# One fused two-block program on one core: modulation rows moved between the projection units, stick-breaking norms moved into the differential attention, opening reordered

## The reference

```python
h = rms_norm(x, g_attn)                      # opening
proj = h @ w_in                              # six outputs of width 512: dq dk dv sq sk sv
dq, dk = rms_norm(dq, qn_g), rms_norm(dk, kn_g)
w = softmax(dq1 dk1 + bias) - lam * softmax(dq2 dk2 + bias)
o_da = rms_norm(w @ dv, subln_g)             # differential attention, 4 heads
o_sb = rms_norm(stick_breaking(sq, sk, sv), sb_out_g)     # 8 heads
x = x + concatenate([o_da, o_sb]) @ w_o
x = x + hier_moe(rms_norm(x, g_ffn), ...)    # 32 experts
# second block
mod = silu(c) @ w_ada + b_ada                # 1024 x 6144, for c and for c_ctx
... modulate(...), Fourier mix, latent attention, feed-forward ...
```

## Time and profile before

| | |
|---|---|
| median of 3 runs | 1538.5 us |
| the profiled execution | 1539.48 us; span 1537.7 us; 1.8 us lie around the span |
| TensorE busy | 1434.8 us (93%) |
| VectorE, ScalarE busy | 526.2 us, 427.2 us |
| mean granted TensorE clock | 0.976 |
| bytes moved | 313.87 MB, mean 204 GB/s |

### The profile page before, as it was taken

The page is one execution under the profiler, slowest core; times in us unless marked ns, Lnnn a source line. Parts: engine busy times, 40 slices in busy tenths (PEclk is TensorE's granted clock), DMA queues, the critical chain, the costliest instruction groups (busy, mean ns, idle before and its releaser), DMA issues.

```text
span 1537.7 us, 16696 instructions
## 1 busy us (share of the span) xinstructions
PE 1434.8 (93%) x6918; PEld 910.6 (59%) x6918; DVE 526.2 (34%) x965; ACT 427.2 (28%) x725; POOL 33.0 (2%) x84
## 2 busy tenths in 40 slices
PE   6999998796999999998999879999999999999996
PEld 5877754484454445444454343555447888887885
DVE  3235557535311211121121045267344222223233
ACT  5237644512100000000200143156334222223222
POOL 0001100000000000000000021000000000000000
PEclk9999999698999999999999999999999999999998
DMA  7421069325699999999999751200004223212201
GB/s 293 135 89 55 1 256 427 165 107 221 273 426 429 427 427 428 427 399 409 394 403 416 286 195 59 79 28 1 0 0 181 93 110 110 89 75 110 83 0 55
DMA packets 30196, 313.87 MB, mean 204 GB/s; under 512 B 3908, under 2 KB 3908, under 8 KB 12456
## 3 DMA queue, kind: packets, MB, share of 16 engines
q1 hardware_dynamic: 22312, 295.06, 46.9%
q10 hardware_dynamic: 6656, 13.53, 2.8%
q0 software_dynamic: 1152, 4.19, 0.8%
HBM read 298.35 MB, written 14.43 MB: 203 GB/s over the span
## 4 chain that ended last, share of the span: by engine, by line
PE 79%; DMA 14%; DVE 3%; ACT 2%; issue 1%; POOL 0%; SPq 0%; ACTq 0%; DVEq 0%; POOLq 0%
PE ps L55 76%; DMA ring<-in_w 7%; DMA B<-in_w 3%; DMA ring<-in_w_ada 2%; PE ps L1061 2%; DMA X<-in_x 1%; PE ps L805 0%; DMA B<-yslots,SMI 0%; POOL B L524 0%; PE ps L571 0%; DVE TMP L1855 0%; DVE WL L1650 0%; DVE X L1653 0%; ACT WH L1559 0%; PE ps L768 0%
## 5 line engine op out<-in xcount | busy, mean ns | idle before, releaser
L55 PE MATMUL ps<-ring,B 128*64 128x512 f32 (+2 forms) x880 | 263.6, 600 | 16.4 <-DMA ring<-in_w 14.7
L55 PEld LDWEIGHTS ps<-ring,B 128*64 128x64 f32 (+1 forms) x880 | 88.2, 147 | 137.9 <-issue 133.6
L55 PE MATMUL ps<-B 128*64 128x512 f32 (+5 forms) x440 | 146.6, 562 | 7.7 <-DMA ring<-in_w 5.9
L55 PE MATMUL ps<-B,B 128*128 128x128 f32 (+1 forms) x1072 | 141.5, 293 | 3.9 <-DVE B L1910 3.9
L55 PE MATMUL ps<-XH,WH 128*128 128x512 f32 (+1 forms) x368 | 140.9, 383 | 1.3 <-DVE XL L1650 0.7
L55 PEld LDWEIGHTS ps<-B,B 128*128 128x128 f32 (+1 forms) x1072 | 123.4, 191 | 28.6 <-issue 24.2
L55 PE MATMUL ps<-XL,WH 128*128 128x512 f32 (+1 forms) x368 | 139.7, 380 | 0.0
L55 PE MATMUL ps<-XH,WL 128*128 128x512 f32 (+1 forms) x368 | 139.7, 380 | 0.0
L1559 ACT ACTIVATE WH<-ring 128x2048 fp32r<-128x2048 f32 x33 | 63.2, 1916 | 168.1 <-PE ps L55 168.1
L1650 DVE TENSOR_TENSOR WL<-ring,WH 128x2048 fp32r<-128x2048 f32 x33 | 75.7, 2293 | 95.4 <-ACT WH L1559 95.4
L1390 ACT ACTIVATE TMP<-ps 64x512 f32<-64x512 f32 x32 | 19.0, 595 | 238.1 <-PE ps L55 238.0
(11 more groups left out here) (293 smaller groups left out, 2012.2 us busy)
## 6 DMA issues: line engine op xcount, KB each, us to landing
ring<-in_w SPq DMA_DIRECT2D x65, 2048.0 KB, 16.9
B<-in_w SPq DMA_DIRECT2D x24, 2048.0 KB, 17.4
ring<-in_w_ada SPq DMA_DIRECT2D x12, 2048.0 KB, 12.6
ring<-in_w_gu SPq DMA_DIRECT2D x11, 2048.0 KB, 8.3
ring<-in_w_in SPq DMA_DIRECT2D x7, 2048.0 KB, 8.8
TO<-in_w SPq DMA_DIRECT2D x7, 2048.0 KB, 16.9
ring<-in_w_down SPq DMA_DIRECT2D x5, 2048.0 KB, 7.2
yslots<-TMP ACTq DMA_DIRECT2D x64, 128.0 KB, 9.2
```

The source lines that it names most:

```text
L55: return e.matmul(o, l, r, start=first, stop=last, skip_group_check=True)
```

## The change

It has four parts.

1. The twelve modulation blocks leave the differential attention. A table `ADA_AT` puts block b behind projection unit n, and its four transposes into unit n+1 (two thirds or three quarters through). They use PSUM bank 7 instead of 5 and 4; `sk` and `dv` therefore use banks 4, 5, 6, 3.
2. The loads of `w_in`, `w_ada` and `w_o` are interleaved in one list and use slots 0, 1, 2 and 4, in the fixed order `early`. The zero source for the overflow slots moves from slot 4 to `B1`, and ScalarE issues its 15 copies two per unit instead of one.
3. The stick-breaking norms (`so_square`, `wo_norm`, `so_norm`, `so_gain`, `so_high`, `so_low`), `od_low(0..1)`, and the first two output weight splits stand inside the passes of the differential attention.
4. In the opening, VectorE squares row tiles 1 and 3, tile 2 is scaled on ScalarE, the transposes go by row tile instead of by column chunk, the first weight split stands ahead of `HH`, the two bias-row matmuls stand behind unit 0, and the parameter load moves from ScalarE's queue to SyncE's, behind `X`.

```diff
+    ADA_AT = {1: 0, 2: 1, 3: 2, 5: 3, 6: 4, 7: 5, 9: 6, 10: 7, 11: 8, 12: 9, 13: 10, 14: 11}
+    early = [0, 1, 2, 4, 1, 0, 2, 4, 0, 2, 1, 4, 2, 1, 0, 4, 1, 2, 1, 2]
...
+        e.dma_start(PRM[:, 0:N_PARAM], I["PRM"]).then_inc(prm_in, 16)
+        for i in range(4):
             load(i)
...
+        def ada_product(b):
+            w = slot(I_ADA[b], 8, 512)
+            if b:
+                e.wait_ge(ada_mod, 2 * b - 1)
+            else:
+                e.wait_ge(cs_set, 4)
+                e.wait_ge(brow_cp, 2)
+            e.wait_ge(slot_in[where[I_ADA[b]]], landed[I_ADA[b]])
+            for c in range(8):
+                m = mm(e, P[7][32 * (c % 4):32 * (c % 4) + 32, :], CS[:, c, :], w[:, c, :], c < 4, c >= 4)
+            m.then_inc(ada_mm, 1)
+
+        def ada_turn(b):
+            e.wait_ge(ada_row, b + 1)
+            for j in range(4):
+                t = e.transpose(P[7][:, 128 * j:128 * j + 128], AD[b % 2][:, 128 * j:128 * j + 128], ident)
+            t.then_inc(ada_T, 1)
...
+                    if c == 5 and n - 1 in ADA_AT:
+                        ada_turn(ADA_AT[n - 1])
...
+            if n in ADA_AT:
+                ada_product(ADA_AT[n])
...
             if i >= 2:
                 qt, h = DA[i - 2]
-                if i - 2 <= 11:
-                    e.wait_ge(ada_mod, 2 * (i - 2) + 1)
...
+                if i in (2, 4, 6, 8):
+                    wo_norm((i - 2) // 2)
+                if i in (10, 14):
+                    turn_rows((i - 10) // 4)
...
-            if i >= 15:
-                wo_norm(i - 15)
-            if i in (14, 15, 17):
-                turn_rows((14, 15, 17).index(i))
+        turn_rows(2)
         out_projection(0)
-        wo_norm(3)
         turn_rows(3)
...
+            if i in (4, 6, 8, 10):
+                so_gain((i - 4) // 2)
+            if i in (6, 8, 10, 12):
+                so_low((i - 6) // 2)
...
+            if i in (12, 16):
+                od_low((i - 12) // 4)
+            if i in (13, 15):
+                wo_low((i - 13) // 2)
```

More of the change, by code:

```diff
@@ L176, in body @@
     ce = small[:, 0:16].rearrange("p (k r) -> p k r", r=2)
-    AD = [B2[:, 2048 + 512 * g:2560 + 512 * g] for g in range(3)]
+    AD = [TMP[:, 2048 + 512 * g:2560 + 512 * g] for g in range(2)]
     E = [[TMP[:, 1024 * k + 512 * j:1024 * k + 512 * j + 512] for j in range(2)] for k in range(3)]
@@ L284, in body @@
     SG = [TMP[:, 2048 + 512 * k:2560 + 512 * k] for k in range(2)]
-    items = [I["w_in"][m] for m in PROJ]
-    I_ADA = len(items)
-    items += [I["w_ada_2"][b] for b in range(12)]
+    items, I_PROJ, I_ADA = [], [], {}
+    for n in range(24):
+        if n % 4 == 0:
+            I_PROJ.append(len(items))
+            items.append(I["w_in"][PROJ[n // 4]])
+        if n in ADA_AT:
+            I_ADA[ADA_AT[n]] = len(items)
+            items.append(I["w_ada_2"][ADA_AT[n]])
+    ada_of = {i: b for b, i in I_ADA.items()}
     I_WO = len(items)
@@ L305, in body @@
     where, before, landed = [], [], []
-    line_up, count = [0, 1, 2], [0] * (NSLOT + 3)
+    line_up, count = [], [0] * (NSLOT + 3)
+    early = [0, 1, 2, 4, 1, 0, 2, 4, 0, 2, 1, 4, 2, 1, 0, 4, 1, 2, 1, 2]
     for i in range(len(items)):
-        line_up = {I_EXP + 1: [4], I_EXP + 4: [3], I_EXP + 5: [NSLOT + 2, NSLOT + 1, NSLOT]}.get(i, []) + line_up
-        if i == I_ADA:
-            line_up = [1, 2, 0]
+        if i < I_EXP:
+            line_up = [early[i]]
+        if i == I_EXP:
+            line_up = [0, 4, 1, 2, 3, NSLOT + 2, NSLOT + 1, NSLOT]
         if i == I_IN2:
@@ L449, in sync @@
         e.wait_ge(brow_out, 16)
-        for i in range(3, I_ADA + 2):
+        for i in range(4, I_EXP):
             e.wait_ge(*consumed(before[i]))
@@ L457, in sync @@
         e.wait_ge(dn_mm, 8)
[L458 to L461, removed]
+        load(I_EXP)
         load(I_EXP + 1)
@@ L690, in out_projection @@
                 e.wait_ge(so_lo, 2 * n + 2)
+            if n == 0:
+                e.wait_ge(da_max, 47)
             if n == 2:
@@ L1174, in scalar @@
         for t in range(4):
-            e.wait_ge(x_in[t], 16)
-            e.activation(junk, X[:, t, :], ACT.Square, accum_out=ss[:, t:t + 1]).then_inc(x_rstd, 1)
-            e.wait_ge(x_rstd, 3 * t + 1)
+            if t % 2:
+                e.wait_ge(x_sq, t // 2 + 1)
+            else:
+                e.wait_ge(x_in[t], 16)
+                e.activation(junk, X[:, t, :], ACT.Square, accum_out=ss[:, t:t + 1]).then_inc(xs_act, 1)
+                e.wait_ge(xs_act, t // 2 + 1)
             ln(rs[:, t:t + 1], ss[:, t:t + 1], 1024).then_inc(x_rstd, 1)
-            e.wait_ge(x_rstd, 3 * t + 2)
+            e.wait_ge(x_rstd, 2 * t + 1)
             rsqrt(rs[:, t:t + 1]).then_inc(x_rstd, 1)
-        e.wait_ge(x_rstd, 12)
-        for k in (1, 3):
-            e.activation(xn[:, k, :], X[:, k, :], ACT.Identity, scale=rs[:, k:k + 1]).then_inc(xn_act, 1)
+            if t == 2:
+                e.wait_ge(x_rstd, 6)
+                e.activation(xn[:, 2, :], X[:, 2, :], ACT.Identity, scale=rs[:, 2:3]).then_inc(xn_act, 1)
         def proj_high(n):
-            w, u = slot(n // 4, 8, 512), n % 4
+            w, u = slot(I_PROJ[n // 4], 8, 512), n % 4
             src = w[:, 2 * u:2 * u + 2, :] if n // 4 in (2, 3) else w[:, :, 128 * u:128 * u + 128]
             if u == 0:
-                e.wait_ge(slot_in[where[n // 4]], landed[n // 4])
+                e.wait_ge(slot_in[where[I_PROJ[n // 4]]], landed[I_PROJ[n // 4]])
             if n >= 2:
@@ L1205, in scalar @@
                 e.activation(ce, cc, ACT.Exp, scale=-1.0).then_inc(cs_exp, 1)
-            if n:
-                e.dma_start(ydram[CAP * (NE + n - 1):CAP * (NE + n), :], ZERO).then_inc(zero_out, 16)
+            if 1 <= n <= 8:
+                for q in range(2 * n - 2, min(2 * n, NOVF)):
+                    e.dma_start(ydram[CAP * (NE + q):CAP * (NE + q + 1), :], ZERO).then_inc(zero_out, 16)
             proj_high(n + 1)
@@ L1656, in vector @@
         e.memset(epsc, EPS).then_inc(eps_set, 1)
-        for k in (0, 2):
-            e.wait_ge(x_rstd, 3 * k + 3)
+        for j, k in enumerate((0, 1, 3)):
+            if j < 2:
+                t = 2 * j + 1
+                e.wait_ge(x_in[t], 16)
+                if j:
+                    e.wait_ge(x_sq, 1)
+                e.tensor_tensor_reduce(JX, X[:, t, :], X[:, t, :], 1.0, 0.0, ALU.mult, ALU.add, ss[:, t:t + 1]).then_inc(x_sq, 1)
+            e.wait_ge(x_rstd, 2 * k + 2)
             e.tensor_scalar(xn[:, k, :], X[:, k, :], rs[:, k:k + 1], None, ALU.mult).then_inc(xn_dve, 1)
```

169 lines of the change are left out of this document (84 added, 85 removed).

## The result

The changed kernel takes **1548.4 us** (median of 9 runs, 1545.2 to 1550.5) against 1538.5 (9 runs, 1535.5 to 1543.3) for the kernel before: a ratio of 1.0063, with a 95% interval from 1.0048 to 1.0077. It is slower by 9.9 us or 0.6%, more than the 3.1 us that the prediction called no change. The forecast was 1542, with a range of its own of 1538 to 1546 and 1534 to 1549 for 8 in 10. The direction had the largest of the three chances (0.45); the size lies outside the forecast's own range and 0.6 us inside the wide one. The profiled execution took 1547.6, 8.1 us more than that of the kernel before.

The account below looks back on a forecast made before the run. Bound by TensorE in the projections, by loads only from about 219 to 268 us, then by small dependent steps to 307. 1539.5 + 30.1 - 26.5 = 1543.1 profiled, forecast 1542 us; own range 1538 to 1546, 8 in 10: 1534 to 1549.

Parts of the forecast that it names:

- half clock through the passes: Rival: TensorE at half clock in all differential attention passes, total 1554.5 us, with one recovery 1549; chance 0.12.
- Step 1: Projection stage: no idle time there, so the twelve moved modulation blocks add their TensorE time in full, +28.8 us.
- The free half of the DMA time: Projection stage: DMA share of only 0.44, taken as evidence against a weight load coming late.
- The rival of a late slot: Rival: a load slot comes late in the projection stage, one wait about 5 us, total 1547; chance 0.05.
- Step 2: Projection stage: TensorE waits for `CS` behind unit 1, +1.1 us, and bias-row matmuls behind unit 0 cost +0.7.
- Step 3: Opening: transposes by row tile let projection unit 0 start earlier, -0.5 us (from -1.5 to +1).
- the case I had set against it: Opening: spread transposes leave TensorE idle, so unit 0 may start at half clock and give the 1.5 us back.
- Step 4: Differential attention through the output units, without blocks: 61.5 + 46.8 = 108.3 us against 134.8, -26.5.
- my layout: Count of all 18 differential attention passes to output unit 0: 57.3 us at full clock, 74 at half clock.
- The first rival: Clock stays full in the differential attention passes: stage 101.6 us, -33.2, total 1535.4; chance 0.20.
- the rule that I weighed: Passes: halved clock is default, sustained activity lifts it, idle time drops it; alone it gives full clock.
- Step 5: Everything behind `x1`: expert loads keep slots and order, no change expected.

Follow-up runs that it names:

- experiment 3: The changed kernel with four instead of eight matmuls in each modulation product: 1540.9 us, ratio 1.0004 to the kernel before.
- experiment 4: The changed kernel with each modulation product done twice into the same bank (16 matmuls in place of 8): 1569.1 us, ratio 1.0196 to the kernel before.
- experiment 8: The changed kernel with unread matmuls filling TensorE's waits in the differential attention passes: 1543.7 us, ratio 1.0028 to the kernel before.
- experiment 5: The changed kernel with the old opening (transposes by column chunk, bias-row matmuls ahead of unit 0): 1546.1 us, ratio 1.0033 to the kernel before.
- experiment 1: The kernel before with only the stick-breaking norms and their splits moved inside the passes, modulation blocks left there: 1525.9 us, ratio 0.990.
- experiment 7: The kernel before with only the norms moved inside the passes, measured again as partner to one with the new opening: 1524.6 us, ratio 0.9906.

## Why the prediction came out as it did

The mechanism was right: a stage of TensorE without a gap pays for the blocks in full, and the stage that they leave gives back less. What was off is the size, by steps (profiled executions, of which each kernel has one):

| step | forecast | measured |
|---|---|---|
| 1 twelve blocks | +28.8 | +30.9 |
| 2 wait for `CS`, bias rows | +1.1, +0.7 | +1.0, +1.2 |
| 3 opening | -0.5 | +0.8 (start -1.0, half clock +1.8) |
| sum before stick-breaking | +30.1 | +33.9 |
| 4 first S to `x1` | -26.5 | -27.9 |
| 5 behind `x1` | 0 | +2.1 (within the scatter) |
| total | +3.6 | +8.1 |

That 1548.4 lies inside the wide range is in part luck. Its upper end was there for half clock through the passes ("with one recovery 1549"), and the passes took the time forecast; the excess came from the projection stage, whose main term had been bounded at 28.2 to 29.3, from the opening, and from behind `x1`.

**Step 1 was mis-sized by 2.1 us.** From product 0 (35.14) to the copies at 142.52 are 107.4 us, where the kernel before has 76.4 from the start of unit 2 (21.25 + 2 x 5.46) to its copies: 30.9, or 2.58 a block. I had added the product and the transposes of the earlier trace rows, 2.35 in all, and up to 0.1 for a switch; by experiments 3 and 4 the matmuls themselves are 1.7, and transposes and switches 0.9. VectorE's 1.05 us a block hid, as forecast.

**The loads** were no wait in the profiled execution of the changed kernel, as forecast, but the argument for it was too easy. "The free half of the DMA time" became a share of 0.81, and experiments 3 and 8 had late weight blocks. The sum of sixteen blocks left out the zero copies and the next weight blocks: 310 GB/s for 122.5 us are 38.0 MB, about eighteen blocks of 2 MB. And the slack was counted "from block 3 on", while the tight load is the weight block of units 4 to 7: it is issued behind product 0 at 37.18, lands at 45.7, and ScalarE splits it at once; this is the one that came late in both experiments. The rival of a late slot did not happen, but was nearer than 0.05 says.

**Step 2** held: the path through the bias rows, `UH` and `UL` ended where it was counted out; TensorE shows 0.76 us of idle time there and a switch. The bias matmuls hold unit 1 up by 1.16 (27.48 to 28.64), the upper end of what I gave them.

**Step 3 had the sign wrong.** The start came 1.0 earlier, but the case I had set against it ("if unit 0 now starts at half clock it gives the 1.5 back") is nearly what happened: the transposes are done by 16.5, TensorE waits for 3.77 us up to 20.23, and the clock falls 1.0 us into unit 0, which then runs some 3.4 us at half clock. In experiment 5, with the transposes right ahead of it, unit 0 runs at full clock. I had also read the slow bias matmuls (2.29 us) and transposes (5.42 us) of the old opening as half clock; the granted clock in the windows from 9 to 21.25 of that profile is 1.00, so this reading is not shown.

**Step 4 was right in its sums, less so in its parts.** Output unit 0 started 61.4 us after the first S (61.5 forecast), and the eight units with their start took 45.5 (46.8). A pass at 512 keys without a norm step takes 3.5 us from S to S (257.41 to 260.91), near the 3.4 counted. But the passes with a norm step do not follow VectorE: in three of the four the norm matmul waits for ScalarE's square (L1319), which my layout did not name, for 1.19 to 1.32 us. Two rows of the timeline of TensorE show the bubble at the start and one of these waits:

```profile
253.58 1.11 PE L770 MATMUL ps<-CST,TMP 128*128 128x128 f32 x4 [2.34 <-DVE TMP L1674]
...
263.67 1.09 PE L55 MATMUL ps<-B,CST 128*128 128x512 f32 x2 [1.19 <-ACT B L1319]
```

The clock was at half for 3.5 us around the end of the bubble, for 3.4 us from 280.5, and in the last six passes, where the layout had the last eight. Passes 10 and 14 also hold `turn_rows` between T and O, which the section on the change leaves out. That 61.5 was met to 0.1 us with these differences in it is in part luck. The -26.5 also takes the norms and the blocks together; priced apart, as experiment 1 does it, they would have shown that the norms alone are the gain. The layout's other figure, 57.3 at full clock, was tested by experiment 8: 57.8. The first rival, full clock and 101.6 for the stage, describes that kernel (102.1) and not this one. As to the rule that I weighed, that the clock falls behind idle time (the Trainium skill, TensorE: Matmul & The Clock Gate, Part 1): behind the bubble at 253.58 TensorE is never idle for longer than 1.32 us in the passes, and the clock still stood at half for 20 us. So the trace disagrees with a reading by long gaps alone; that filling the short waits held the clock up agrees with the rule that activity lifts it.

**Step 5 came out 2.1 us longer, which is not shown to be the change.** From `x1` to the end of the span the kernel before takes 1189.3 us and the changed one 1191.5. But experiments 1 and 7, the same kernel twice, take 1190.8 and 1187.6, and all eleven profiles lie between 1185.3 and 1194.5. About half of the 2.1 us lies where the experts begin. The clock is low while the router keeps TensorE idle, in both kernels. The first 64 matmuls of the experts begin 5.6 us ahead of its rise in the changed kernel (377.3 to 382.9) and 3.3 ahead of it in the one before (371.3 to 374.6), and take longer. In the chain of the changed kernel and of the kernel before:

```profile
377.26 10.13 PE ps L55 x64
```
```profile
371.26 9.00 PE ps L55 x64
```

The same 64 matmuls take 9.07 us in experiment 1 and 9.91 in experiment 7, so this too differs within one kernel. The last 1.0 lies in the expert stages, where the clock falls for some microseconds at a few places (608 and 943 us, which the kernel before did not have). Why it falls there, and whether the change has a part in it, stays open; so do 1.8 us by which the medians differ more than the two profiles, within the interval.

**Where the gain went.** Experiment 1 answers it. With the norms inside and the blocks left in, the passes to output unit 0 take 71.6 us; taking the blocks out makes them 61.4. So 10.2 us are gained for 30.9 paid, since the blocks had been filling TensorE's waits in the passes and kept its clock up. Of what the norms win (16.4 us up to `x1`), 9.6 are left once the blocks no longer stand there. The loads that I had read as the bound of the old stage do stand on its chain, but TensorE was busy beside them for nine tenths of the time (44.27 of the 48.50 us from 219.5 to 268) and waited for them 4.2 us in all, so little was to be won behind that wait.

## What to carry to other kernels

A wait that ends a chain says what is late, not what its removal is worth: look at how full the next engine is in the same window before moving its work elsewhere. Work that fills an engine's short waits costs a part of its time there (here 10.2 us for 28.2 us of matmuls) and its full time, plus its switches, in a stage without gaps (30.9). When one change holds several parts, try each alone: here one part won 1%, and another lost more than that.

## What was not expected of the hardware

- A block of 8 + 4 matmuls in the middle of a stream of another kind costs 2.56 us in a steady unit (8.02 - 5.46), of it 0.88 for four transposes and the switches, where the four transposes alone are 0.35 to 0.49.
- Unread matmuls in TensorE's waits shortened a kernel by 4.8 us in that stage, though they stand in the same queue as the work.
- Starting unit 0 of the projections 2.2 us earlier (20.23 against 22.40) let it end only 0.4 us earlier, since the clock fell to half 1.0 us into it and it took 7.25 us. In all six profiles with the new opening TensorE waits 2.6 to 3.8 us ahead of unit 0 and the clock is at half in it; in the five with the old opening it follows the transposes directly and stays at full clock.
